# Recurrence streams stored per stream, with two pairs side by side in each chunk

## The chip, the cores and the metric

One core of one Trainium2 chip runs the kernel. The metric is device time in microseconds (us) for one execution. The engines are PE (TensorE), DVE (VectorE), ACT (ScalarE), POOL (GpSimd) and SP (SyncE), and 16 DMA engines move data between DRAM and the on-chip memory (SBUF). DMAs issued by SP go out on the DMA queue q1, those issued by POOL on q0, and instructions are fetched on q8.

## The reference

A two-block network on 512 tokens (and 256 context tokens), width 1024. The part that matters here is the first mixer, an RWKV-7 layer with 16 heads of 64, scanned forwards and backwards:

```
def wkv_scan(r, w, k, v, kk, a, s0, reverse):
    def step(S, inp):
        r_t, w_t, k_t, v_t, kk_t, a_t = inp
        sa = jnp.einsum("bhvk,bhk->bhv", S, kk_t)
        S = (S * w_t[:, :, None, :]
             - sa[..., None] * (kk_t * a_t)[:, :, None, :]
             + v_t[..., None] * k_t[:, :, None, :])
        return S, jnp.einsum("bhvk,bhk->bhv", S, r_t)
```

`rwkv7_streams` makes r, v, kk, the decays, a and kd from one projection of the normed input; `rwkv7_readout` norms the outputs, adds a bonus, gates with silu(g) and projects. A differential attention layer, and two layers of a hybrid attention (block sparse, dilated, memory), follow. All of it is float32.

## The kernel before

The kernel is written engine by engine, with explicit semaphores, in five stages: `Mix`, `Scan`, `Mid`, `Diff`, `Second`. A barrier (`to_scan`) stands between Mix and Scan. All streams are laid out with 128 channels (a pair of heads) on the partitions; there are 8 pairs (`gp`), and 768 tokens = 6 tiles of 128 = 12 chunks of 64.

**Mix.** For each pair, `project(gp)` multiplies four weight blocks (each split into a high and a low part: ACT writes `wah`, line 238, and POOL writes `wal`, line 243, and PE's product waits for `wal`), and `post(gp)` makes nine streams in one SBUF tile `S9` of [128, 9, 768]. Their order is b, kd of the forward direction (0, 1), v (2), b, kd of the backward direction (3, 4), kk and r of the forward direction (5, 6), kk and r of the backward direction (7, 8). `together` interleaves `post(gp)` with `project(gp + 1)` on each engine by hand. There are two `S9` tiles, used in turn. At the end of `post(gp)` POOL waits for DVE's last product (`prd_v`, line 935) and issues six stores, one for each tile of 128 tokens, each of 128 partitions x 9 pieces of 512 bytes, into the DRAM tensor `str`. POOL's next `wal` stands behind them in its order. When `project(gp + 2)` comes to its second mix, ACT first waits in `stored` (line 694) until the six stores of pair `gp` have landed (semaphore at 96 per use), because they read the same `S9`. Another store per pair, `bg`, issued on the same queue, takes the gate and the bonus.

**Barrier.** After the last pair POOL waits at lines 1046 and 1047 for all stores, and only then SP issues the masks `rc` and the first fetch of Scan.

**Scan.** Four groups `g` of two pairs each are scanned in six rounds, so 24 rounds `u`. Each round takes one tile of the forward and one of the backward direction. `sp_fetch` loads it: for each direction d and pair q, one DMA takes b, kd and v into `bkv` (128 x 6 pieces of 256 bytes, because the chunks of the two pairs alternate in `bkv`) and one takes kk and r into `ARI` (128 x 2 pieces of 512 bytes). That makes 8 DMAs per round, and `fetched` waits for 8 x 16 = 128 on one of two semaphores. The fetch of round u is issued when PE has used `bkv` of round u - 2 (line 1157) and when `ARI` of round u - 4 is free. In rounds below 12, SP also loads two blocks of `wm` of 512 KB, and in six rounds one `bg` tile of 768 KB. PE's work of three rounds (prepare, invert, chain) is interleaved by `pace`.

Of the kernel before, what the change touches and what calls it, by code (L numbers as in the profile page):

```python
# [584 lines left out]
class Mix:  # L585
# [332 lines left out]
    def pool_post(self, e, gp):  # L918
        K, s, u = self.K, self.K.s, gp % 2
        S9 = self.s9[u]  # L920
        yield
        yield
        if gp:
            self.pool_bonus(e, gp - 1)
        yield
        yield

        e.wait_ge(s.dec_a, 4 * gp + 4)
        for d in range(2):
            m = e.tensor_copy(K.pcA[:, gp, 12 * d:12 * d + 12], self.er[:, d, 64 - 64 * d:780:65])  # L930
        m.then_inc(s.prd_p, 1)
        yield
        yield
        yield
        e.wait_ge(s.prd_v, 8 * gp + 8)
        e.wait_ge(s.mix_done, 5 + 3 * gp)
        for n in range(6):
            e.dma_start(K.T["str"][gp, n], S9[:, :, 128 * n:128 * n + 128]).then_inc(self.st_out[u], 16)
        yield

    def pool_bonus(self, e, gp):
# [121 lines left out]
class Scan:  # L1063
# [89 lines left out]
    def sp_fetch(self, e, u):  # L1153
        K, s, w, g, i = self.K, self.K.s, u % 2, u // 6, 2 * (u % 4)
        if u >= 2:

            e.wait_ge(s.pp_mm, self.pp_use[u - 2] + 5)
        if u >= 4:

            e.wait_ge(*self.iv_at(u - 4, v=7))  # L1160
        for d in range(2):
            src = K.T["str"][2 * g:2 * g + 2, self.tile(u, d)].rearrange("q p n t -> p q n t")
            for q in range(2):
                e.dma_start(self.bkv[:, w, d, :, :, q, :], src[:, q, 2 * d:2 * d + 3, :].rearrange(
                    "p n (c t) -> p n c t", c=2)).then_inc(self.scan_in[w], 16)
                e.dma_start(self.ARI[:, q, i:i + 2, 128 * d:128 * d + 128],
                            src[:, q, 5 + 2 * d:7 + 2 * d, :]).then_inc(self.scan_in[w], 16)

    def fetched(self, e, u):
        e.wait_ge(self.scan_in[u % 2], 128 * (u // 2 + 1))  # L1170

    def stream(self, u, i, d):

# [1939 lines left out]
```

## Time and profile before

| | us |
|---|---|
| median of 3 runs | 2658.24 (2657.24 to 2663.86) |
| the profiled execution, its own time | 2653.53 |
| its span in the profile | 2651.7 |
| Mix, until the barrier opens | about 0 to 497.8 |
| Scan | about 498 to 1200 |

The span runs from the first to the last instruction. PE is busy in 84% of it, DVE in 52%, ACT in 44%, POOL in 25%. A busy share is an average over stages with different limits, so each stage is read by itself. The granted clock of TensorE over the whole is 0.927 of full speed.

### The profile page before, as it was taken

The page shows a single profiled execution, that of the slowest core. Times are in us where ns is not written, and L with a number is a line of the kernel's source. Part 1 is how long each engine was busy: PE and PEld are TensorE (multiplying, and loading weights), DVE is VectorE, ACT ScalarE, POOL GpSimd, SP SyncE. Part 2 cuts the span into 40 slices and gives each one's busy share as a digit, 9 for nine tenths or more (in the row PEclk, how much of TensorE's full clock was granted, in tenths as well). Part 3 has the DMA queues.
Part 4 walks back from the last instruction along what each step waited for, and adds up shares of the span by engine and source line. Part 5 has one row for each costly group of instructions (what it writes and reads, how often), then busy time and mean ns, then how long its engine had stood idle before and what let it go on. Part 6 is the DMA issues. An engine that isn't in the chain of part 4 may idle for free.

```text
span 2651.7 us, 59035 instructions
## 1 busy us (share of the span) xinstructions
PE 2239.0 (84%) x25736; PEld 1640.2 (62%) x25736; DVE 1372.8 (52%) x2342; ACT 1160.5 (44%) x1933; POOL 667.8 (25%) x410
## 2 busy tenths in 40 slices
PE   8799998389888878876898888977899888898988
PEld 2577776167667767664765665654666555665656
DVE  1358788244344544444266565562455653455552
ACT  2466676143333433332254444442354453444452
POOL 0334444200011010113232222213423332433332
PEclk9899999599988999997999999987999998999998
DMA  7115454642431222222221111102111111111111
GB/s 267 57 61 174 131 162 120 181 122 75 121 94 49 65 72 61 61 68 100 84 86 36 36 33 39 34 22 86 59 55 56 56 56 57 63 56 56 48 64 64
DMA packets 148481, 211.32 MB, mean 80 GB/s; under 512 B 81920, under 2 KB 106752, under 8 KB 147456
## 3 DMA queue, kind: packets, MB, share of 16 engines
q1 hardware_dynamic: 137120, 164.28, 19.5%
q0 software_dynamic: 9952, 40.11, 5.0%
q8 instruction: 204, 3.34, 0.5%
q10 hardware_dynamic: 1152, 3.15, 0.3%
q14 instruction: 53, 0.43, 0.1%
HBM read 165.30 MB, written 42.21 MB: 78 GB/s over the span
## 4 chain that ended last, share of the span: by engine, by line
PE 59%; DVE 19%; ACT 10%; issue 7%; POOL 3%; DMA 2%; SPq 0%; ACTq 0%; DVEq 0%; POOLq 0%
PE ps L258 7%; PE ps L260 7%; PE ps L259 7%; PE ps L1332 3%; PE ps L538 2%; PE ps L311 2%; PE ps L1322 2%; PE ps L1347 2%; PE ps L2706 2%; PE ps L2233 2%; PE ps L391 2%; PE ps L2729 1%; PE ps L2715 1%; DVE st L2292 1%; DVE p L2306 1%
## 5 line engine op out<-in xcount | busy, mean ns | idle before, releaser
L243 POOL TENSOR_TENSOR wbl<-wb,wbh 128x1024 fp32r<-128x1024 f32 x128 | 306.3, 2394 | 603.0 <-ACT wbh L238 597.8
L258 PE MATMUL ps<-hT2h,wbh 128*128 128x512 f32 x416 | 189.9, 456 | 23.9 <-POOL wbl L243 16.5
L258 PE MATMUL ps<-hTh,wah 128*128 128x512 f32 (+1 forms) x512 | 180.6, 353 | 17.3 <-POOL wal L243 10.9
L258 PE MATMUL ps<-hT1h,wbh 128*128 128x512 f32 (+1 forms) x432 | 178.8, 414 | 3.1 <-POOL hT1l L2372 3.1
L259 PE MATMUL ps<-hTl,wah 128*128 128x512 f32 (+1 forms) x512 | 174.8, 341 | 0.0
L260 PE MATMUL ps<-hTh,wal 128*128 128x512 f32 (+1 forms) x512 | 174.7, 341 | 0.0
L260 PE MATMUL ps<-hT2h,wbl 128*128 128x512 f32 x416 | 169.5, 408 | 0.0
L259 PE MATMUL ps<-hT2l,wbh 128*128 128x512 f32 x416 | 169.4, 407 | 0.0
L238 ACT ACTIVATE wbh<-wb 128x1024 fp32r<-128x1024 f32 x128 | 134.6, 1052 | 68.8 <-PE ps L1928 43.5
L339 POOL TENSOR_TENSOR ro<-ro 128x256 f32<-128x256 f32 (+1 forms) x12 | 11.9, 993 | 580.6 <-DVE ro L323 580.6
L243 POOL TENSOR_TENSOR wal<-wa,wah 128x1024 fp32r<-128x1024 f32 x34 | 102.3, 3011 | 219.3 <-ACT wah L238 219.3
L260 PE MATMUL ps<-hT1h,wbl 128*128 128x512 f32 (+1 forms) x432 | 157.2, 364 | 0.0
L259 PE MATMUL ps<-hT1l,wbh 128*128 128x512 f32 (+1 forms) x432 | 157.0, 363 | 0.0
L1434 ACT ACTIVATE DE<-ps 128x512 f32<-128x512 f32 x96 | 57.3, 597 | 209.9 <-PE ps L1332 209.9
L1482 DVE COPY_PREDICATED Y<-rc,ps 128x512 f32<-128x512 int32 x120 | 86.1, 736 | 113.0 <-ACT DE L1434 79.3
L258 PEld LDWEIGHTS ps<-hTh,wah 128*128 128x128 f32 x512 | 99.7, 195 | 42.0 <-issue 17.5
L258 PEld LDWEIGHTS ps<-hT2h,wbh 128*128 128x128 f32 x416 | 83.0, 200 | 57.0 <-issue 22.1
L2715 PE MATMUL ps<-con,pc 128*128 128x128 f32 x304 | 62.0, 306 | 53.9 <-DVE pc L2790 53.9
L259 PEld LDWEIGHTS ps<-hTl,wah 128*128 128x128 f32 x512 | 99.9, 195 | 10.9 <-issue 1.4
L260 PEld LDWEIGHTS ps<-hTh,wal 128*128 128x128 f32 x512 | 99.7, 195 | 10.6
L258 PEld LDWEIGHTS ps<-hT1h,wbh 128*128 128x128 f32 x432 | 83.0, 192 | 35.4 <-issue 20.1
L2253 ACT ACTIVATE p<-ps,st 128x768 f32<-128x768 f32 x64 | 57.7, 902 | 91.1 <-DVE st L2296 83.4
(400 smaller groups left out, 5704.9 us busy)
## 6 DMA issues: line engine op xcount, KB each, us to landing
wb<-in_w_in SPq DMA_DIRECT2D x56, 512.0 KB, 3.4
s_str_dram<-s POOLq DMA_DIRECT2D x48, 576.0 KB, 8.7
wm<-in_ada SPq DMA_DIRECT2D x48, 512.0 KB, 4.5
bkv<-s_str_dram SPq DMA_DIRECT2D x96, 192.0 KB, 3.4
wa<-in_rw_in SPq DMA_DIRECT2D x34, 512.0 KB, 4.2
wb<-in_da_in SPq DMA_DIRECT2D x32, 512.0 KB, 3.4
ARI<-s_str_dram SPq DMA_DIRECT2D x96, 128.0 KB, 3.5
wb<-in_w_out SPq DMA_DIRECT2D x16, 512.0 KB, 3.5
```

Of the source, the lines that this page charges most:

```text
L238: e.activation(self.hi[:, n % 2], self.raw[:, n % 3], ACT.Copy).then_inc(self.K.s.w_hi, 1)
L243: e.tensor_tensor(self.lo[:, n % 2], self.raw[:, n % 3], self.hi[:, n % 2].bitcast(F32), ALU.subtract).then_inc(self.K.s.w_lo, 1)
L258: e.matmul(z, wh[:, k, :], hi[:, k, a:b], start=k == 0, stop=False)
L259: e.matmul(z, wh[:, k, :], lo[:, k, a:b], start=False, stop=False)
L260: m = e.matmul(z, wl[:, k, :], hi[:, k, a:b], start=False, stop=k == 7)
L311: e.matmul(m, lhs, sq, start=True, stop=True).then_inc(self.ss, 1)
L391: m = e.matmul(self.K.psum[:, self.banks[j], 0:b - a], self.K.ones, self.rows[k % self.n][:, a:b], start=k == 0, stop=k == 7)
L1332: m = e.matmul(ps[half(h), x + c, blk64(2 * d + q)], self.L[half(c), w, j, blk64(2 * d + p)], rhs, start=True, stop=True)
L1434: e.activation(self.DE[:, u % 2, 1 - l % 2, :, 256:512], banks[:, :, 256:512], ACT.Copy).then_inc(a, 1)
L1482: e.copy_predicated(self.Y[:, l - 1], twice(self.mY[l - 1]), banks[:, :, 0:256]).then_inc(v, 1)
L2253: e.activation(self.p[cc][z % 3][:, :], psum[:, 4 + 2 * cc:6 + 2 * cc, :].rearrange("p a n -> p (a n)")[:, 0:768], ACT.Exp, scale=0.125, b ...
L2715: m = e.transpose(psum[:, 7 if i % 2 else 3, 128 * y:128 * y + 128], self.pr[i % 4][:, 128 * y:128 * y + 128], K.ident)
```

## The change

The DRAM tensor `str` now holds only b, kd and v, with one block per stream, and within a partition the 12 chunks, and within a chunk the two pairs of a group side by side. kk and r go into a tensor of their own, `sar`. Each pair still issues six stores, but they are different ones: five, one per stream, of 128 partitions x 12 pieces of 256 bytes (each at a distance of 512 bytes from the next), and one of 128 partitions x 12288 bytes. In Scan the fetch of b, kd and v for both pairs is now one DMA per direction, of 128 x 3 pieces of 1024 bytes. The fetches of `ARI` keep their 128 x 2 pieces of 512 bytes. A round issues 6 DMAs in place of 8, and `fetched` waits for 96.

```
-        for n in range(6):
-            e.dma_start(K.T["str"][gp, n], S9[:, :, 128 * n:128 * n + 128]).then_inc(self.st_out[u], 16)
+        for n in range(5):
+            e.dma_start(K.T["str"][gp // 2, n, :, :, u, :], self.by_chunk(S9[:, n, :])).then_inc(self.st_out[u], 16)
+        e.dma_start(K.T["sar"][gp], S9[:, 5:9, :]).then_inc(self.st_out[u], 16)
...
-            src = K.T["str"][2 * g:2 * g + 2, self.tile(u, d)].rearrange("q p n t -> p q n t")
+            n = self.tile(u, d)
+            e.dma_start(self.bkv[:, w, d].rearrange("x s c q t -> x s (c q t)"),
+                        K.T["str"][g, 2 * d:2 * d + 3, :, 2 * n:2 * n + 2].rearrange("s x c q t -> x s (c q t)")).then_inc(
+                self.scan_in[w], 16)
             for q in range(2):
-                e.dma_start(self.bkv[:, w, d, :, :, q, :], src[:, q, 2 * d:2 * d + 3, :].rearrange(
-                    "p n (c t) -> p n c t", c=2)).then_inc(self.scan_in[w], 16)
                 e.dma_start(self.ARI[:, q, i:i + 2, 128 * d:128 * d + 128],
-                            src[:, q, 5 + 2 * d:7 + 2 * d, :]).then_inc(self.scan_in[w], 16)
+                            K.T["sar"][2 * g + q, :, 2 * d:2 * d + 2, 128 * n:128 * n + 128]).then_inc(self.scan_in[w], 16)
...
-        e.wait_ge(self.scan_in[u % 2], 128 * (u // 2 + 1))
+        e.wait_ge(self.scan_in[u % 2], 96 * (u // 2 + 1))
...
-    for k, shape in (("str", (8, 6, 128, 9, 128)), ("bg", (8, 128, 2, 768)),
+    for k, shape in (("str", (4, 5, 128, 12, 2, 64)), ("sar", (8, 128, 4, 768)), ("bg", (8, 128, 2, 768)),
```

## Rows read from the trace of the kernel before

**Rows 1.** The chain that ended last, around one pair's stores: start us, us, what
```profile
280.24 5.97 POOL s_str_dram L938 x6
286.21 2.42 POOL wal L243
...
299.97 0.71 ACT s L661
300.68 0.95 ACT wah L238
```

**Rows 2.** The same chain at the barrier
```profile
478.65 2.40 POOL s_str_dram L938 x3
481.05 0.01 issue
481.05 2.39 POOL s_str_dram L938 x2
483.44 13.07 DMA s_bg_dram<-gbuf
...
504.04 3.72 DMA ARI<-s_str_dram
507.76 0.14 issue
507.90 1.95 PE ps L1197 x8
```

**Rows 3.** PE's waits, us 150 to 480: in total, times, longest
```profile
PE ps L258 <- POOL wal L243: 10.9, 6, 2.5
```

**Rows 4.** POOL's timeline: start us, us; the last column is idle before
```profile
237.08 5.96 POOL L938 DMA_DIRECT2D s_str_dram<-s  x6 [8.38 <-DVE s L916]
241.94 3.49 POOL L243 TENSOR_TENSOR wal<-wa,wah 128x1024 fp32r<-128x1024 f32 x1
...
248.43 0.57 POOL L945 DMA_DIRECT2D s_bg_dram<-gbuf  x1
```

**Rows 5.** DMA queues alone on stores, us 481 to 492: packets, MB, share
```profile
q0 software_dynamic: 784, 2.91, 97.9%
```

**Rows 6.** DMA queues with a weight load beside the stores, us 294 to 296
```profile
q1 hardware_dynamic: 111, 0.42, 83.9%
q0 software_dynamic: 98, 0.34, 42.4%
```

**Rows 7.** Windows, core 0: us, busy of each engine, PEclk, DMA share, GB/s
```profile
193.90:195.30 1.40, 1.40 (x8) 1.16 (x7) 0.62 (x2) 0.51 (x1) 1.40 (x2) 1.00 0.05 12
...
481.00:492.00 11.00, 0.00 (x0) 0.00 (x0) 0.00 (x0) 0.00 (x0) 4.17 (x5) 0.50 0.98 264
...
1000.00:1000.60 0.60, 0.60 (x38) 0.60 (x38) 0.00 (x0) 0.13 (x1) 0.00 (x0) 1.00 1.10 440
```

**Rows 8.** Six stores of the first pair, then of the fourth, and their landing
```profile
L938 POOL DMA_DIRECT2D s_str_dram<-s x6: 1122/1404/1905, 193.9 to 198.1; - x6
...
DMA to landing us min/median/max: 4.7/8.7/13.7
...
L938 POOL DMA_DIRECT2D s_str_dram<-s x6: 976/1422/1926, 323.5 to 327.5; - x6
...
DMA to landing us min/median/max: 4.6/8.7/13.8
```

**Rows 9.** ACT's timeline: the first write into the `S9` tile stored before
```profile
213.31 1.12 ACT L661 ACTIVATE s<-pad,omu 128x256 f32<-128x256 f32 x2
...
257.84 1.12 ACT L661 ACTIVATE s<-pad,omu 128x256 f32<-128x256 f32 x2
...
342.75 1.12 ACT L661 ACTIVATE s<-pad,omu 128x256 f32<-128x256 f32 x2
```

**Rows 10.** DMA queues in one fetch of Scan, us 502 to 506.5, then 1013.7 to 1020.4
```profile
DMA packets 4123, 1.31 MB, mean 291 GB/s; under 512 B 3176, under 2 KB 4115, under 8 KB 4119
...
q1 hardware_dynamic: 4123, 1.31, 117.5%
...
q1 hardware_dynamic: 4215, 1.31, 80.9%
q8 instruction: 2, 0.03, 2.3%
```

**Rows 11.** The timeline in one fetch of Scan
```profile
1014.12 0.55 SPq L1166 DMA_DIRECT2D ARI<-s_str_dram  x1
...
1014.97 0.53 PE L1235 MATMUL ps<-vax,LK 64*64 64x64 f32 x24
1015.22 1.91 SPq L1166 DMA_DIRECT2D ARI<-s_str_dram  x1
...
1018.04 0.34 PE L1235 MATMUL ps<-vax,LK 64*64 64x64 f32 x7 [2.53 <-issue]
```

**Rows 12.** PE's waits in Scan (us 560 to 1160), and waits for a fetch (484 to 520)
```profile
PE ps L1235 <- issue: 19.3, 7, 3.8
PE ps L1358 <- DVE oT L1503: 13.7, 6, 4.3
...
PE ps L1197 <- DMA ARI<-s_str_dram: 31.8, 1, 31.8
```

**Rows 13.** Pieces of the chain above 1 us with no releaser, us 560 to 1160: first, last of 14
```profile
618.32 1.32 issue
...
1110.46 1.65 issue
```

## The prediction

> **What bounds the kernel now.** I read the chain that ended last first, then the waits, then DMA windows. The change touches two stages. In Mix the chain leaves DVE's last product, passes through POOL's six stores (5.97 us) into POOL's next `wal`, from there into PE's product, and later through ACT's `s` at line 661 [rows 1]. PE's waits confirm it: six times it stood still until `wal` came, 10.9 us in all [rows 3]. So whatever POOL takes longer over its stores, PE waits longer, in six pairs. At the end of Mix no arithmetic is left: the stores of the last pair are issued at 478.65 and the barrier waits for the last landing, at 483.44 + 13.07 = 496.5 [rows 2]. The DMA engines are 98% busy in between [rows 7], so this stretch is DMA throughput. Then the first fetch lands at 507.8 and Scan starts [rows 2]. In Scan that first fetch is the only one that PE waits for by name [rows 12]; all others are issued about a round ahead. But in the middle of a fetch PE halts after 24 of the 32 matmuls of one group, for 2.53 us and for no dependency [rows 11], and the instruction queue q8 shows two packets in that stretch, on the engines that carry the fetch [rows 10]. I read that as instructions that arrive late. At line 1235 it happens seven times, 19.3 us [rows 12]. The chain holds 14 pieces above 1 us in which it waited for nothing [rows 13]; the 12 that lie inside a fetch sum to 26 us, my estimate of what is exposed.
>
> **POOL's issue.** A store of 128 x 9 = 1152 pieces keeps POOL for 5.96 / 6 = 0.99 us, one of 128 pieces for 0.57 us [rows 4]: 0.42 us for 1024 pieces more. The new stream store has 1536 pieces: 0.57 + 1408 x 0.00041 = 1.15 us. Five of them and one of 128 pieces: 5.75 + 0.57 = 6.3 us, against 5.96: +0.4 us a pair, and 6 pairs on the path give +2.4 us. Bounds: if pieces cost nothing beyond 1152, 5.5 us (-0.4 a pair, -2.4 in all); if time goes in proportion, 7.2 us (+1.2, +7.4). The Trainium skill ("DMA: Bandwidth & Descriptors", section on the anatomy of a DMA issued from GpSimd) calls descriptor generation small and says many can be emitted before a cost shows. By it this term would be nothing; the 0.99 against 0.57 us [rows 4] say otherwise, and I use them.
>
> **The price of a 256-byte piece in a store.** This decides the case, and no row shows one. Now 2.91 MB in pieces of 512 bytes take 97.9% of 16 engines for 11 us: 172 us / 5680 pieces = 30.3 ns each [rows 5]. At the rate of the large pieces, 440 / 1.10 = 400 GB/s [rows 7], 512 bytes would be 20.5 ns and 256 bytes 10.2 ns. Beside a weight load, the same pieces take 42.4% x 2 us x 16 / 664 = 20.4 ns [rows 6]. So they can move at the full rate when another queue fills the gaps; alone, they wait for something that comes once per piece, every 30 ns. If that holds, a piece of 256 bytes alone takes 30 ns too. Per pair and engine there are now 432 pieces, 432 x 30.3 = 13.1 us. After: 480 small pieces, and 1.57 MB of kk and r at 400 GB/s, 3.9 us:
> at 10.2 ns (bytes at the full rate) 8.8 us (-4.3), the lower bound; at 20.1 ns (30.3 less the bytes saved) 13.5 us (+0.4); at 30.3 ns 18.4 us (+5.3), which I take, because of rows 6; at twice that, the upper bound, 33.0 us (+19.9).
>
> **Where it shows.** (a) The tail before the barrier is that time itself: +5.3 us. (b) In six pairs ACT waits in `stored`. The first pair's stores land at 198.1 + 13.7 = 211.8, ACT writes at 213.31: 1.5 us of slack; the fourth's land at 327.5 + 13.8 = 341.3, ACT writes at 342.75: 1.4 us [rows 8, 9]. Counted from the first issue, they land 17.9 us on, and ACT needs them 19.3 to 20.8 us on (213.3 - 193.9; 257.8 - 237.1). The 17.9 are 1.4 of start [rows 7], 13.1, about 2.6 for 1.05 MB of weights, and 0.8 for the completion. After: 1.4 + 0.2 + 18.4 + 0.8 = 20.8; the weights now fill gaps, from 0 to 2.6 of them stay, I take 0.7: 21.5. Less the 0.4 by which everything behind POOL has moved, ACT waits 1.8 us in four pairs and 0.3 in two, less in the last, which has no weights beside it: +7 us. What is late next is `wah`, then `wal`, then PE [rows 1]. The `bg` store, last on the queue, is waited for only at the fourth product two pairs on, some 10 us later, and stays hidden. PE's clock is already 0.50 (1.2 GHz) in the tail [rows 7], so a longer tail costs none there.
>
> **Scan.** A fetch moves 1.31 MB in 4123 packets and takes 117.5% x 4.5 x 16 = 84.6 us of engine time; the bytes at 400 GB/s are 52, so a piece adds 7.9 ns [rows 10]. After, 768 pieces of 1 KB at 41 + 8 and 1024 of 512 bytes at 20.5 + 8 ns are 67 us: 1.1 us less on the 16 engines, 21%. For the first fetch, where this and two issues fewer are on the path, I take -1 us (0 to -2.5: `rc` is ahead of it either way). The other 23 are covered by PE's work of a round; without that cover each would be worth the same 1.1 us. What they may give is shorter instruction stalls: nothing at one end (the instruction packet waits behind what is queued when it is asked for, and that is no less at the start of a fetch), all 26 us at the other. I take the share of the DMA time, 21%: -6 us.
>
> **Sum.** +2.4 + 5.3 + 7 - 1 - 6 = +7.7 us. The profiled execution took 2653.5 us (span 2651.7, 1.8 around it), 4.7 below the median of the runs; I add the change to the median: 2658.2 + 7.7 = 2666 us.
>
> **Rivals.**
> 1. *The small write costs double, 60 ns* (0.15). Landing 1.6 + 33.0 + 0.8 = 35.4 us on; ACT then waits some 15 us in each of six pairs, 91 us, the tail grows by 20, with +2.4, -1 and -6: +106 us, 2764 us. At 45 ns (landing at 27.9, 46 us of waits, tail +12.4) it would be +54, 2712 us. For it: no store below 512 bytes exists in this trace. Against it: pieces of 256 bytes into SBUF add only 8 ns [rows 10]. The Trainium skill (the same page, "Specifications") says that below 512 bytes a transfer is a read-modify-write; by that rule this rival comes true.
> 2. *Bytes count, not pieces* (0.25). At about 20 ns the landing stays within the slack of 1.4 us: +2.4 + 0.4 - 1 - 6 = -4 us, 2654 us, no change that can be told. For it: only that the excess of a 512-byte piece, 10 ns, could be a fixed addition; rows 6 speak against.
> 3. *Faster: the instruction stalls go* (0.15). They stand at the end of fetches' first 2 us; SP's issue itself blocks there (1.91 us for one that else takes 0.55 [rows 11]). If a shorter fetch with 6 issues lets the instruction packet through in time, 20 of the 26 us come back, and with pieces near 20 ns the sum is +2.4 + 0.4 - 1 - 20 = -18, 2640 us. It decides from 10 us of relief at 20 ns on, or from 22 us at 30 ns.
> 4. *The change does nothing for the fetch*: relief 0 with 30 ns, +13.7 us, 2672 us; it is the upper half of my own case.
>
> **Chances.** My case (30 ns, relief 0 to 12 us; 2660 to 2672 us) 0.45. The time of no change and mine are close: 0.3% of 2658 us is 8 us, about what a measurement of this kernel can tell from none, and my sum sits just inside. I put half of my case on each side. Slower: 0.15 + 0.23 of mine + 0.04 of rival 2 = 0.42. Same: 0.22 of mine + 0.18 of rival 2 = 0.40. Faster: 0.15 + 0.03 of rival 2 = 0.18. The range goes from 2640 us (rival 3) to 2712 us (45 ns); below and above it are 0.05 and 0.15.
>
> **What would show it.** In the profile after, POOL's six stores take 6.3 us; between 481 and the barrier the queue q0 runs near 16 x 256 / 30.3 = 135 GB/s and then at 400; the barrier opens 5 us later; ACT waits for `s_str_dram` in pairs two to seven. If that rate is 200 GB/s or more, rival 2 holds; if it is 70, rival 1. In Scan the packets of a fetch fall from 4100 to about 1800, and PE's idle time at line 1235 with no releaser tells relief from none. I am wrong above all if the price of the small piece is not 30 ns: each ns is worth 0.5 us in the tail, and another 0.5 in each of six pairs once the 1.4 us are gone.

## The result: the time was met, the steps behind it were not

| | us |
|---|---|
| before, median of 20 runs | 2657.61 (2650.12 to 2664.46) |
| after, median of 20 runs | 2665.32 (2656.31 to 2675.91) |
| ratio after / before | 1.0028, 95% interval 1.0017 to 1.0038 |
| the profiled execution of after | 2656.85, span 2655.0, granted clock 0.924 |

The forecast was 2666 us. The kernel is 0.28% slower, 7.5 us at 2658 (4.5 to 10 by the interval). Almost none of the steps that led to 2666 can be found in the profile after: the stage that should have grown by 13.7 us (Mix, with its tail and the first fetch) did not grow, and the stage that should have shrunk by 6 us (Scan) became longer. The errors cancelled.

**Packets.** The page of after, DMA part: packets and MB of the whole, then by queue, and the issues of the changed tiles.

```profile
DMA packets 90368, 211.31 MB, mean 80 GB/s; under 512 B 7424, under 2 KB 50688, under 8 KB 88320
...
q1 hardware_dynamic: 81056, 164.28, 18.6%
q0 software_dynamic: 7904, 40.11, 5.3%
...
bkv<-s_str_dram SPq DMA_DIRECT2D x48, 384.0 KB, 4.5
...
s_str_dram<-s POOLq DMA_DIRECT2D x40, 384.0 KB, 7.5
s_sar_dram<-s POOLq DMA_DIRECT2D x8, 1536.0 KB, 14.4
```

The bytes are the same and the change did what it says: one `bkv` load now carries 384 KB, and of 81920 packets below 512 bytes 7424 are left. (The store queue counts few packets because each holds many pieces, so its pieces are worked out from bytes below.)

**POOL's stores.** The timeline of POOL in after, at the first pair: start us, us, idle before.

```profile
192.61 5.20 POOL L938 DMA_DIRECT2D s_str_dram<-s  x5 [8.38 <-DVE s L916]
197.34 1.02 POOL L939 DMA_DIRECT2D s_sar_dram<-s  x1
197.91 2.84 POOL L243 TENSOR_TENSOR wal<-wa,wah 128x1024 fp32r<-128x1024 f32 x1
```

From 192.61 to 198.36 the stores take 5.75 us, and 5.6 us at the second pair, where [rows 4] had 5.96 and the forecast 6.3. Less 0.57 us for the store of 128 pieces, a store of 1536 pieces costs about 1.02 us, where one of 1152 cost 0.99.

**Landing.** ACT's timeline of after, where it first writes into the tile that was stored; [rows 9] has 213.31 for it.

```profile
212.16 0.58 ACT L651 ACTIVATE pad<-ps 128x512 f32<-128x512 f32 x1
212.83 1.12 ACT L661 ACTIVATE s<-pad,omu 128x256 f32<-128x256 f32 x2
```

The last store of that pair into `str` or `sar`, the one of kk and r, lands 14.4 us after its issue at 197.3, at 211.7, and ACT comes at 212.83 with no idle time before it. The slack is 1.1 us. The predicted wait in `stored` is not there, in this pair or another. PE's waits of after in Mix, us 150 to 480 (total, times, longest), stand against [rows 3]:

```profile
PE ps L258 <- POOL wal L243: 8.8, 6, 2.2
```

**The tail and the first fetch.** First the chain that ended last in after, then two windows of the tail (us, busy of each engine, PEclk, DMA share, GB/s), then the queue in the first of them; they answer to [rows 2, 5, 7].

```profile
475.73 2.17 POOL s_str_dram L938 x3
477.90 0.55 issue
478.45 2.33 POOL s_str_dram L938 x2
480.78 0.01 POOL s_sar_dram L939
480.79 13.64 DMA s_bg_dram<-gbuf
...
499.00 5.37 DMA ARI<-s_sar_dram
504.37 0.14 issue
504.50 1.95 PE ps L1199 x8
```

```profile
478.00:487.00 9.00, 0.00 (x0) 0.00 (x0) 0.00 (x0) 0.00 (x0) 3.87 (x5) 0.50 0.97 201
487.50:491.00 3.50, 0.00 (x0) 0.00 (x0) 0.00 (x0) 0.00 (x0) 0.00 (x0) 0.50 1.00 401
```

```profile
q0 software_dynamic: 495, 1.81, 97.2%
```

From the first issue to the landing of the last store it is 494.43 - 475.73 = 18.7 us, against 496.51 - 478.65 = 17.9 before: +0.8 us, where +5.3 was forecast. In the first window the pieces of 256 bytes move at 201 GB/s: 1.81 MB are 7070 pieces, and 97.2% of 16 engines for 9 us is 140 us, so 19.8 ns a piece. The last microsecond of the window already holds some packets of kk and r. Without it (us 478 to 486) the queue moved 1.53 MB at a share of 96.1%, which is 5980 pieces at 20.6 ns. The 512-byte piece took 30.3 ns in the same place [rows 5]. If the time of a piece is a fixed part and the bytes on top, half the bytes took 9.7 to 10.5 ns less, which is 256 bytes at 24 to 26 GB/s for one engine, and leaves 9 to 11 ns that come with any piece. The large pieces bear the slope out: 401 GB/s are 25 GB/s for one engine.

From the landing to the first matmul of Scan it is 10.1 us, against 11.4: -1.3 us, where -1 was forecast. It has two parts. From the landing to the last issue of the fetch it is 4.6 us (494.43 to 499.00) against 7.5 before, because SP issues six DMAs and not eight; from there to the first matmul it is 5.5 us against 3.9 [rows 2].

**Scan.** PE's waits of after, us 560 to 1160, against [rows 12]:

```profile
PE ps L1237 <- issue: 20.1, 7, 4.8
...
PE ps L1334 <- issue: 7.4, 5, 2.3
PE ps L1349 <- issue: 7.3, 7, 2.2
```

The idle time of PE with no releaser sums to 38.9 us over all its lines there; the same view of before sums to 34.8. The fetch that [rows 10, 11] show of before, in after: the queues between us 1015 and 1021.2, then SP's and PE's timeline.

```profile
DMA packets 1890, 1.34 MB, mean 217 GB/s; under 512 B 96, under 2 KB 1888, under 8 KB 1888
...
q1 hardware_dynamic: 1888, 1.31, 79.3%
q8 instruction: 2, 0.03, 2.2%
```

```profile
1014.02 0.36 SPq L1164 DMA_DIRECT2D bkv<-s_str_dram  x1
1014.43 1.01 SPq L1168 DMA_DIRECT2D ARI<-s_sar_dram  x2
1015.48 0.47 SPq L1164 DMA_DIRECT2D bkv<-s_str_dram  x1
1015.99 1.00 SPq L1168 DMA_DIRECT2D ARI<-s_sar_dram  x2
...
1016.47 0.53 PE L1237 MATMUL ps<-vax,LK 64*64 64x64 f32 x23
1019.63 0.34 PE L1237 MATMUL ps<-vax,LK 64*64 64x64 f32 x8 [2.64 <-issue]
```

The fetch is cheaper in engine time, but by less than forecast: 79.3% x 6.2 us = 4.9 us on 16 engines, against 117.5% x 4.5 = 5.3 us and 80.9% x 6.7 = 5.4 us before [rows 10]. That is 7 to 9%, not 21%. SP puts it out in 3 us, where its eight issues took about 5.7 (us 1012.61 to 1018.27). And the halt in the middle of a group is still there, 2.64 us against 2.53 [rows 11].

**Where the 7.5 us are.** From the first stream store to the first matmul of Scan it is 314.0 us before and 311.9 after, the same again in a second execution of after (below): -2.1 us. e4 below, whose code is that of before up to there, has 313.1, so this gain is 1 to 2 us. From `QG`'s first to its last instruction (before, then after), the body of Scan, it is 638.8 us before and 642.5 after.

```profile
L1490 DVE TENSOR_TENSOR QG<-ps,ARI x24: 1224/1225/1225, 556.7 to 1195.5; 128x1024 f32<-128x1024 f32 x24
...
L1492 DVE TENSOR_TENSOR QG<-ps,ARI x24: 1223/1225/1225, 553.4 to 1195.9; 128x1024 f32<-128x1024 f32 x24
```

Behind Scan nothing differs but scatter (1455 to 1459 us in all the kernels of this study). The profiled executions are single ones and lie below their medians by different amounts, and the scatter of Scan is as large as the difference. So the size comes by subtraction: Scan should hold some +9.6 us (7.5 + 2.1).

### The profile page after: what moved, and what is told of

Same layout as the page of the kernel before. It is cut to its first block, busy times and chain, and to the rows that moved or that the text cites. A ratio compares the mean times of both kernels' runs of the same rounds, so it can differ in the third digit from the quotient of the medians.

```text
span 2655.0 us, 58987 instructions
## 1 busy us (share of the span) xinstructions
PE 2241.7 (84%) x25736; PEld 1642.4 (62%) x25736; DVE 1371.8 (52%) x2342; ACT 1161.5 (44%) x1933; POOL 665.7 (25%) x410
## 2 busy tenths in 40 slices
DMA packets 90368, 211.31 MB, mean 80 GB/s; under 512 B 7424, under 2 KB 50688, under 8 KB 88320
## 3 DMA queue, kind: packets, MB, share of 16 engines
q10 hardware_dynamic: 1152, 3.15, 0.3%
## 4 chain that ended last, share of the span: by engine, by line
PE 60%; DVE 19%; ACT 9%; issue 7%; POOL 3%; DMA 2%; ACTq 0%; SPq 0%; DVEq 0%; POOLq 0%
PE ps L258 7%; PE ps L259 7%; PE ps L260 7%; PE ps L1334 3%; PE ps L538 2%; PE ps L1324 2%; PE ps L311 2%; PE ps L1349 2%; PE ps L2708 2%; PE ps L2235 2%; PE ps L391 2%; PE ps L2731 1%; PE ps L2717 1%; DVE st L2294 1%; DVE p L2308 1%
## 5 line engine op out<-in xcount | busy, mean ns | idle before, releaser
L258 PEld LDWEIGHTS ps<-hTh,wah 128*128 128x128 f32 x512 | 99.9, 195 | 39.9 <-issue 17.5
L259 PEld LDWEIGHTS ps<-hTl,wah 128*128 128x128 f32 x512 | 100.1, 195 | 10.9 <-issue 1.4
## 6 DMA issues: line engine op xcount, KB each, us to landing
s_sar_dram<-s POOLq DMA_DIRECT2D x8, 1536.0 KB, 14.4
```

The source lines that it names most:

```text
L258: e.matmul(z, wh[:, k, :], hi[:, k, a:b], start=k == 0, stop=False)
L259: e.matmul(z, wh[:, k, :], lo[:, k, a:b], start=False, stop=False)
```

## The experiments

"Scan" is from the start of the first to that of the last `QG <- ps,ARI` instruction; "halts" is PE's idle time with no releaser, us 560 to 1160, all lines; both come from one profiled execution. "Held" means that a load is issued later than its buffer allows. The ratio is to the kernel before, timed on the same chip. Scatter of Scan between executions of one kernel is up to some 10 us, that of the halts up to 9, so the ratios decide.

| kernel | ratio (95%) | Scan | halts |
|---|---|---|---|
| before | 1 | 638.8 | 34.8 |
| after | 1.0028 (1.0017 to 1.0038) | 642.5 | 38.9 |
| e1, after again | 1.0028 (1.0013 to 1.0044) | 652.5 | 39.6 |
| e2, loads of 512-byte pieces | 0.9999 (0.9985 to 1.0013) | 635.1 | 30.5 |
| e11, e2 again | 1.0005 (0.9986 to 1.0024) | 642.2 | 39.9 |
| e5, loads in partition halves | 1.0010 (0.9994 to 1.0026) | 644.9 | 36.3 |
| e12, e5 again | 1.0026 (1.0011 to 1.0042) | 650.6 | 37.9 |
| e4, before, fetch held | 0.9947 (0.9925 to 0.9968) | 625.2 | 27.8 |
| e3, after, fetch held | 0.9937 (0.9914 to 0.9959) | 627.0 | 27.1 |
| e6, e3, one store a pair | 0.9985 (0.9971 to 0.9999) | 628.7 | 29.8 |
| e8, e6, `wm` held too | 0.9961 (0.9948 to 0.9975) | 608.4 | 28.8 |
| e9, whole rows stored | 0.9930 (0.9909 to 0.9950) | 637.3 | 38.2 |
| e7, e9, fetch held | 0.9890 (0.9868 to 0.9913) | 621.2 | 28.0 |
| e10, e7, `wm` held too | 0.9865 (0.9843 to 0.9886) | 621.6 | 27.3 |

### e1: the changed kernel again

No edit.

> The changed kernel once more, for a second profile. Theory A (the loss is in Scan: PE's instructions arrive later because the new fetch queues more bytes ahead of them): ratio about 1.003; PE's idle time with no releaser between 560 and 1160 us is 37 to 42 us, against 34.8 in the first profile of before, and the first fetch starts Scan 2 to 4 us earlier than in before. Theory B (the loss is in Mix or after Scan, Scan is as it was): the second profile shows Scan (from the first matmul of line 1199 to the last QG) no longer than before's 688 us.

1.0028 again, and the tail, the stores and PE's wait for `wal` (8.8 us) repeat to 0.1 us. Scan was 10 us longer than in the first execution with nearly the same halts; its granted clock was 0.87 in us 700 to 850, against 0.92. So what is called slower here is real, and a single profile of Scan can't give its size.

### e2 and e11: the new stores, loads in pieces of 512 bytes

```
+                e.dma_start(self.bkv[:, w, d, :, q].rearrange("x s q t -> x s (q t)"),
+                            K.T["str"][g, 2 * d:2 * d + 3, :, 2 * n + q].rearrange(...))
...
-        e.wait_ge(self.scan_in[u % 2], 96 * (u // 2 + 1))
+        e.wait_ge(self.scan_in[u % 2], 128 * (u // 2 + 1))
```

In the loop over `q` in place of the one load of 1 KB pieces: eight issues a fetch again.

> The new stores, but each bkv fetch of a direction split in two by chunk, so 8 DMAs a round again, with 3 pieces of 512 bytes per partition. Theory A: the DMAs are again small and issued over the same 5 us as before, so PE's idle time with no releaser falls back to about 35 us or less; Mix keeps its gain of 1 to 3 us; the ratio to before is 0.998 to 1.000. Theory B: as slow as the change, 1.003.

> The second run again (two DMAs by chunk, 3 pieces of 512 bytes each), beside the fifth's kernel on the same chip, since 0.9999 and 1.0010 did not part. Theory P (pace of the issues): both equal within 0.1%. Theory S (size of the piece): this one 0.1 to 0.3% below the next.

0.9999 and 1.0005, with the stores unchanged and PE's wait for `wal` at 9.9 and 9.7 us. Timed on one chip, twelve executions each, e1 is 0.36% above e2 (plus or minus 0.11%). So the new stores cost nothing that can be told, and what makes the changed kernel slower sits in its loads. The two profiles of this one kernel show Scan at 635.1 and 642.2 us, which warns against reading 3.7 us from a pair of profiles.

### e5 and e12: pieces of 1 KB, issued as eight DMAs

```
+                e.dma_start(self.bkv[half(q), w, d].rearrange("x s c q t -> x s (c q t)"),
+                            K.T["str"][g, 2 * d:2 * d + 3, half(q), 2 * n:2 * n + 2].rearrange(...))
```

The load of 384 KB is split by partitions, 192 KB each, so that the number of issues is that of before and the size of a piece that of after.

> The changed kernel with each bkv fetch split into two DMAs by halves of the partitions: pieces of 1 KB as in the change, but 8 DMAs a round of the old size, issued over the old time. Theory P (an instruction packet waits behind the bytes that SP has queued in the time before it, so the pace of the issues counts): like the run with two DMAs by chunk, ratio to before 0.998 to 1.001, PE's idle time with no releaser near 30 us (560 to 1160 us). Theory S (the size of the piece counts, since an instruction packet waits for whole pieces): like the change, ratio 1.003, idle near 39 us.

> The fifth run again (halves of the partitions, pieces of 1 KB). Theory P: as the run before it in this series, 0.999 to 1.001. Theory S: 1.001 to 1.003.

1.0010 and 1.0026. If the denser issue were to blame, this kernel should equal e2; if the larger piece, it should equal after. Both times it lies 0.1 to 0.2% above e2, and the second time at the changed kernel's ratio. Timed on one chip, e12 is 0.22% above e11, plus or minus 0.19%. Its issues are less dense, too: SP puts out one fetch over 5.7 us in e5 and 6.4 in e12, and over 4.0 to 5.0 us in e11 and e2. That leans to the piece, but e5 alone can't be told from e2, and e5 and e12 also halve the partitions of each DMA: the question stays open.

### e3 and e4: the fetch held until the halting group is through

```
-            e.wait_ge(s.pp_mm, self.pp_use[u - 2] + 5)
+            e.wait_ge(s.pp_mm, self.pp_use[u - 2] + 6)
```

In e3 on the changed kernel, in e4 on the kernel before. SP issues the fetch one group of PE's later; nothing else differs.

> The changed kernel with each fetch held until PE has also done the group at line 1237 of two rounds before. Theory A: the seven halts inside that group, 20 us, go, since nothing is on the DMA engines then; if the next instruction packet is late in their place, halts of 1 to 2 us appear in the groups behind it and only some 5 to 10 us are won: ratio to before 0.994 to 1.000. Theory B (the halts come from PE's own instruction stream, not from the fetch): they stay at that line, and the ratio is 1.003.

> The kernel before with the same delay of its fetch. Theory A: its seven halts at line 1235 (19 us) go or get shorter, ratio 0.992 to 0.998. Theory B: they stay, ratio 1.000.

0.9937 and 0.9947: about 14 us off the kernel before and 24 us (1.0028 to 0.9937) off the changed one. The timeline of e3 at the same fetch:

```profile
1005.22 0.53 PE L1237 MATMUL ps<-vax,LK 64*64 64x64 f32 x24
1006.85 0.34 PE L1237 MATMUL ps<-vax,LK 64*64 64x64 f32 x8 [1.10 <-issue]
...
1007.24 0.36 SPq L1164 DMA_DIRECT2D bkv<-s_str_dram  x1
```

PE still halts after the 24th matmul, with no fetch under way, but for 1.10 us and not 2.64. In e4 it is 1.08 us at the same place, against 2.53 [rows 11]. PE's waits in e3, then in e4, us 560 to 1160:

```profile
PE ps L1237 <- issue: 12.9, 7, 4.0
```

```profile
PE ps L1235 <- issue: 12.5, 7, 3.7
```

So at this place a halt has two parts: about 1.1 us that come with the place in the program, and the rest, which comes with the fetch in flight. That PE waits there for its instructions, as the prediction read it, fits both, but no run shows it directly. Held, both kernels have the same halts (27.8 and 27.1 us) and nearly the same Scan (625.2 and 627.0). Timed on one chip, e3 is 0.06% below e4, plus or minus 0.19%, so the 0.28% that the change costs are gone: they arise in this overlap. The halts fell by 7 us and Scan by 13.6 in the kernel before. Weighted over us 560 to 1160, the granted clock was 0.942 before and 0.955 in e4, which is about the size of the rest; no run separates the two, and e1 shows that the clock differs as much between executions of one kernel.

### e6: one stream store a pair, pieces of 256 bytes

```
-        for n in range(5):
-            e.dma_start(K.T["str"][gp // 2, n, :, :, u, :], self.by_chunk(S9[:, n, :]))...
+        e.dma_start(K.T["str"][gp // 2, :, :, u, :], self.by_chunk(S9[:, 0:5, :].rearrange("x n t -> x (n t)")))...
```

On e3, with the loads following the new shape.

> The changed kernel with the late fetch of the third run, and the five stream stores of a pair merged into one of 128 x 60 pieces of 256 bytes (the DRAM tensor has the partition outermost). The third run had ratio 0.9937. If POOL's time for stores is on the path in six pairs: POOL takes about 0.6 + 7552 x 0.0003 = 2.9 us and 0.5 us for kk and r instead of 5.7, PE's waits for wal (8.8 us) shrink to 0 to 3 us, ratio 0.990 to 0.992. If the path only moves to another wait: ratio 0.9937 as before.

0.9985 against 0.9937 for e3: 0.5% lost, which neither of the two expectations had. POOL's timeline of e6 and then ACT's, first pair:

```profile
190.89 2.75 POOL L937 DMA_DIRECT2D s_str_dram<-s  x1 [8.39 <-DVE s L916]
193.60 0.59 POOL L938 DMA_DIRECT2D s_sar_dram<-s  x1
```

```profile
211.31 1.12 ACT L661 ACTIVATE s<-pad,omu 128x256 f32<-128x256 f32 x2 [2.77 <-DMA s_sar_dram<-s]
```

POOL is through in 3.3 us, and PE no longer waits for `wal` at all. But now ACT waits 2.77 us for the store, 8.3 us in three pairs. This is the wait that the prediction described, in another kernel. It has two sources. Counted from the first store, ACT comes after 17.7 us (208.54 - 190.89), where it came after 20.2 us in after, because POOL is off its path; and the store lands after 20.4 us, against 19.1. The windows of e6 in the tail show where the later landing comes from:

```profile
481.00:483.00 2.00, 0.00 (x0) 0.00 (x0) 0.26 (x1) 0.00 (x0) 2.00 (x1) 0.50 0.00 0
483.00:493.00 10.00, 0.00 (x0) 0.00 (x0) 0.00 (x0) 0.00 (x0) 1.46 (x3) 0.50 0.89 178
```

While POOL works on the DMA of 7680 pieces, nothing moves, and the queue stays empty to us 484. Five stores let the first one move while the second is made; one does not. From issue to landing the tail takes 20.2 us, and PE's wait for ACT at line 787 in Mix rises from 5.5 us in after to 20.2. Not all of that is ACT's new wait: in e7 below, where ACT waits for no store, it is 12.2 us, since ACT is what is late next once `wal` comes in time. In e6, then in e7:

```profile
PE ps L787 <- ACT s L830: 20.2, 8, 4.1
...
PE ps L787 <- ACT s L830: 12.2, 8, 2.1
```

### e9, e7: whole rows

```
-        for n in range(6):
-            e.dma_start(K.T["str"][gp, n], S9[:, :, 128 * n:128 * n + 128])...
+        e.dma_start(K.T["str"][gp], S9[:, :, :])...
...
+                for c in range(2):
+                    e.dma_start(self.bkv[:, w, d, :, c, q, :],
+                                src[:, q, 2 * d:2 * d + 3, 64 * c:64 * c + 64])...
```

On the kernel before: `str` is (8, 128, 9, 768), one store a pair of 27,648 bytes a partition, and the fetch is twelve DMAs with `bkv` in pieces of 256 bytes, as small as before. e9 has the fetch at its old place, e7 holds it.

> The seventh run's stores and fetch (one store of whole rows per pair, 12 DMAs a round) without the late fetch, so that its ratio of 0.989 can be divided. If the stores give their share alone (POOL's issue, the waits for wal, the tail): 0.9945 to 0.996, and PE's idle time with no releaser is back at 30 to 36 us. If the late fetch gave nearly all and the stores nothing: 0.999 to 1.001.

> The kernel before with the late fetch, and one store per pair of whole rows (27648 bytes per partition) instead of six; the fetch of b, kd and v then needs two DMAs per direction and pair, of 3 pieces of 256 bytes each, so 12 DMAs a round. POOL takes about 0.6 us for the store, PE's waits for wal (10.9 us) go, the tail before the barrier gets 4 us shorter (3.5 MB at 400 GB/s against 264). Against it: 12 issues take SP 6 us a round, the first fetch starts Scan about 2 us later. Sum against the fourth run (0.9947): 10 to 13 us less, ratio 0.990 to 0.991. Where six pairs' POOL time is not on the path, only the tail is won: 0.994.

0.9930 and 0.9890. POOL's timeline, the windows and the chain of e7:

```profile
190.93 0.74 POOL L937 DMA_DIRECT2D s_str_dram<-s  x1 [8.39 <-DVE s L916]
```

```profile
468.00:476.00 8.00, 0.00 (x0) 0.00 (x0) 0.00 (x0) 0.00 (x0) 0.51 (x1) 0.50 1.04 442
```

```profile
467.98 10.84 DMA s_bg_dram<-gbuf
...
487.32 3.35 DMA ARI<-s_str_dram
490.67 0.14 issue
490.81 1.95 PE ps L1198 x8
```

POOL's 6 us become 0.74, the wait for `wal` is gone, and the stores move at 442 GB/s. Scan starts at 490.8 instead of 507.9, but 3 us of that had been won before the first store, by code that is the same in both. From the first store to the first matmul of Scan it is 299.9 us (300.3 in e9), where it was 314.0: 8.6 us less in Mix, 6.1 less in the tail and 0.6 more in the first fetch. Whole rows in the stores were worth about 14 us before Scan. The 0.7% of e9 is more than its expectation had for the stores alone (0.55% at the most); its Scan (637.3) is that of before within the scatter, though its twelve issues a fetch are twice those of after. Holding the fetch gives 0.4% here as well.

### e8 and e10: the load of `wm` held too

```
             for q in self.chunks(u):
+                if u:
+                    e.wait_ge(K.s.pp_mm, self.x_use(u - 1) + 1)
                 self.mod.load(e, q)
```

On e6 and on e7. With the fetch held, the longest halt of line 1237 was 4.0 us in e3, at us 778, beside loads of `wm` and `bg`.

> The sixth run with the loads of wm in rounds below 12 also held until PE has done line 1236's group of the round before. If the halts that are left between 560 and 850 us (about 14 us in the third run) come from those loads: they fall to 5 to 8 us, and the time is 4 to 8 us below that of the sixth run. If wm is then late for line 538, PE waits for a DMA there, and the time is that of the sixth run or longer.

> The seventh run (0.989) with the loads of wm held as in the eighth run, which was 0.24% below the sixth. If both gains add: 0.986 to 0.987. If the wm loads, now behind 12 issues a round, come late for line 538: 0.989 or above, with PE waiting for a DMA there.

0.9961 after 0.9985, 0.9865 after 0.9890: 0.25% both times, each difference about as large as its intervals. PE's waits of e10, against the 13.0 us with a longest of 4.3 in e7:

```profile
PE ps L1236 <- issue: 10.7, 7, 1.8
```

The longest halt at this line is 1.8 us now. But the halts as a whole hardly fell, from 29.8 to 28.8 us in e8 and from 28.0 to 27.3 in e10; between us 560 and 850, where 14 us were to become 5 to 8 in e8, they are 13.2. So what the 0.25% are is not shown. The 608.4 us for Scan in e8 are no measure of them: its granted clock was 0.98 in us 700 to 850, where e6 had 0.90 and e10 0.93. e10 is the best version of the study, 1.35% faster than the kernel before; its median was 2617.85 us.

## Why the prediction was right in its number and wrong in its reasons

| term | forecast | measured |
|---|---|---|
| POOL's stores | +2.4 | 0 to -2.1 (PE's wait for `wal`, 10.9 to between 8.8 and 10.9) |
| tail | +5.3 | +0.8 |
| ACT's waits in `stored` | +7 | 0 |
| first fetch | -1 | -1.3 |
| Scan's halts | -6 | no relief (34.8 to 38.9 and 39.6, within the scatter), and Scan some 10 us longer |

**The price of a piece in a store** is the first step that failed. The prediction had two readings of 30.3 ns for 512 bytes: a wait that comes once per piece whatever its size, or a fixed part with the bytes on top. It took the first because the same pieces ran at 20.4 ns beside a weight load [rows 6]; the second is what the runs show (19.8 to 20.6 ns), as its rival 2 had it. From [rows 6] only follows that something besides bytes is in the 30.3 ns, not that the bytes are hidden under it; why it took 20.4 ns there stays open. With that price the landing stayed within ACT's slack, and the +7 us of the six pairs became nothing. The mechanism by which ACT would wait was right, and e6 shows it.

**Read-modify-write.** Pieces of 256 bytes cost less than pieces of 512, at the same place in the two kernels: rival 1 (60 ns, +106 us) is out. The Trainium skill ("DMA: Bandwidth & Descriptors", "Specifications") has transfers below 512 bytes as a read-modify-write; a cost of it does not show in the 19.8 to 20.6 ns here. The doubling to 60 ns was the prediction's own assumption.

**POOL's issue** was mis-sized. The line through 128 and 1152 pieces gave 1.15 us for 1536; it is 1.02. e6 has 2.75 us for 7680 pieces, which from 0.57 at 128 is 0.29 ns a piece. e7's store of whole rows, mostly 0.57 us (0.53 to 0.74), shows the 0.57 as about the floor. So the term came out between nothing and its lower bound (-2.4): PE's wait for `wal` is 8.8 us in both profiles of after, and 9.2 to 10.9 in e2, e3, e5, e11 and e12, which have the same stores.

**The first fetch** was right in its number, for half of its reasons. SP's fewer issues gave -3 us up to the last issue, and the way from there to the first matmul grew by 1.6. The engine time of a fetch was mis-sized: with 8 ns on top of the bytes of a packet it should have fallen from 84.6 to 67 us over the 16 engines, and it is 79.3% x 6.2 x 16 = 78.7. With fewer than half the packets, each has 14 ns on top of its bytes ((78.7 - 52) / 1888).

**The relief of the halts** is the second step that failed. The prediction made the halt shorter in proportion to the DMA time of a fetch; that time fell by 7 to 9%, the halts did not fall, and Scan became longer. That the halts rose is not shown: e11 has 39.9 us of them, as many as after, at a ratio of 1.0005. e3 and e4 show that the halts do hang on the fetch in flight, so the mechanism was there; what they depend on is not its total. The issues of after are closer together (6 in 3 us, not 8 in 5.7) and its pieces are larger. e2 and e11 take the slowdown back by splitting the load; e5 and e12, with as many issues as before and the pieces of after, lie in between. Which of the two it is stays open.

**The number.** -2.1 us before Scan where +13.7 was forecast, and by subtraction some +9.6 in Scan where -6 was: two errors of 16 us, one each way. That they cancel is luck. The tell-tales that the prediction named (201 GB/s in the tail, ACT without a wait, no relief of the halts) reject it in spite of the 2665.3.

## What to carry to other kernels

A transfer's small side can be moved from its load to its store, but each side has its own price and its own thing that waits: price the piece where it would go, by a line through two sizes and not by one, and ask whether anything waits for the side that gets better. When a prefetch is hidden, look at what else uses the DMA engines while it runs, the instruction queue first; moving the burst by one group of matmuls was worth more (0.4 to 0.9%) than any change of its pieces (0.3% at the most). A total that comes out right proves no term of it: compare every term, and take a few tenths of a per cent from many timed executions, not from two profiles.

## What was not expected of the hardware

- A store piece of 256 bytes took 19.8 to 20.6 ns where one of 512 took 30.3: about 10 ns and the bytes on top, though the store alone reached only 201 GB/s, and 401 GB/s as soon as only the large pieces were left.
- A DMA that POOL issues moves nothing until POOL is through with it: with 7680 pieces the queue stayed empty for 3 us (us 481 to 484 in e6).
- TensorE stopped in a dense row of 64x64 matmuls for about 1.1 us with no DMA traffic beside it (e3, e4), and for 2.5 to 2.6 us at the same place with a fetch in flight (before, after). The packets of the instruction queue (two in a fetch, 16 KB each) run on the same 16 engines [rows 10].
